# Attention of a two-block kernel: two heads per product, small and large query tiles in turn

## The reference

```
sc = (q_nope . k_nope + q_rope . k_rope) * 96 ** -0.5      # 8 heads, blocks of 128 queries
p = softmax(where(causal, sc, -inf))
out = p @ v                                                # v: 64 columns per head
```

## Time and profile before

| what | value |
|---|---|
| time, median of 3 runs | 2957.47 us (2949.0 to 2968.39) |
| the profiled execution: time, span | 2962.7 us, 2961.0 us |
| busy in the span: PE, DVE, ACT, POOL | 93%, 66%, 46%, 20% |
| attention stage, on the timeline | 1986.8 to 2168.4 us |
| in it, busy: PE, DVE, ACT, POOL | 172.8, 117.9, 89.7, 8.2 us |

### The profile page before, as it was taken

One profiled execution on the slowest core, in us unless ns is written; L12 is line 12 of the kernel. 1 busy time (PEld: TensorE's weight loads), 2 busy tenths in 40 slices (PEclk: granted clock), 3 DMA queues, 4 the chain that ended last, 5 costly groups with the idle time before them and its releaser, 6 DMA issues. The chain is left out here.

```text
span 2961.0 us, 39198 instructions
## 1 busy us (share of the span) xinstructions
PE 2741.1 (93%) x14472; PEld 2268.7 (77%) x14473; DVE 1958.9 (66%) x2494; ACT 1354.4 (46%) x1902; POOL 580.1 (20%) x465
## 2 busy tenths in 40 slices
PE   8999889889979789999999699779999899999998
PEld 7988677777767678888887688657678688888887
DVE  4441167777754689999997843766677888887323
ACT  5111155555542277777776432334455333333312
POOL 0000036555550110000000510320000234331000
PEclk9999989999989799999999899989999899999999
DMA  6446311010007379999997611010031222222314
GB/s 207 178 173 245 113 39 36 36 36 35 27 30 259 128 308 410 409 410 407 411 409 278 186 61 43 1 52 7 0 91 61 64 78 85 85 85 103 140 49 157
DMA packets 165242, 439.27 MB, mean 148 GB/s; under 512 B 21836, under 2 KB 101760, under 8 KB 151808
## 3 DMA queue, kind: packets, MB, share of 16 engines
q1 hardware_dynamic: 150512, 383.60, 35.1%
q0 software_dynamic: 8848, 33.03, 2.9%
q10 hardware_dynamic: 5760, 20.97, 1.7%
HBM read 358.40 MB, written 79.17 MB: 148 GB/s over the span
## 5 line engine op out<-in xcount | busy, mean ns | idle before, releaser
L134 PE MATMUL psum<-part,expert_x_high 128*128 128x512 f32 x520 | 207.0, 398 | 2.9 <-issue 1.5
L136 PE MATMUL psum<-part,expert_x_low 128*128 128x512 f32 x520 | 203.4, 391 | 0.0
L134 PE MATMUL psum<-project_w_high,high 128*128 128x448 f32 (+1 forms) x512 | 194.8, 380 | 3.5 <-DVE low L398 3.5
L135 PE MATMUL psum<-project_w_low,high 128*128 128x448 f32 (+1 forms) x512 | 193.9, 379 | 0.0
L136 PE MATMUL psum<-project_w_high,low 128*128 128x448 f32 (+1 forms) x512 | 193.8, 379 | 0.0
L129 DVE TENSOR_TENSOR expert_down_low<-expert_down,expert_down_high 128x2048 fp32r<-128x2048 f32 x62 | 139.3, 2287 | 39.6 <-ACT expert_down_high L124 39.6
L971 POOL TENSOR_TENSOR mix_ab_step<-mix_abrb,mix_pair_mask 128x512 f32<-128x512 f32 x80 | 116.4, 1479 | 186.1 <-ACT mix_abrb L1106 185.6
L134 PE MATMUL psum<-part,ffn_w_high 128*128 128x512 f32 x352 | 140.5, 399 | 11.6 <-DVE ffn_w_low L129 6.8
L129 DVE TENSOR_TENSOR expert_gate_low<-expert_gate,part 128x2048 fp32r<-128x2048 f32 x64 | 143.8, 2287 | 8.5 <-ACT part L124 7.0
L129 DVE TENSOR_TENSOR expert_up_low<-expert_up,part 128x2048 fp32r<-128x2048 f32 x64 | 143.8, 2288 | 1.0 <-ACT part L124 1.0
L135 PE MATMUL psum<-ffn_b_low,ffn_w_high 128*128 128x512 f32 x352 | 139.1, 395 | 0.0
(11 more groups left out here) (702 smaller groups left out, 7684.7 us busy)
## 6 DMA issues: line engine op xcount, KB each, us to landing
expert_gate<-in_w_gate_dram SPq DMA_DIRECT2D x32, 2048.0 KB, 10.1
expert_up<-in_w_up_dram SPq DMA_DIRECT2D x32, 2048.0 KB, 9.9
expert_down<-in_w_down_dram SPq DMA_DIRECT2D x32, 2048.0 KB, 10.9
ffn_w<-in_ffn_w_up_dram SPq DMA_DIRECT2D x44, 512.0 KB, 4.6
y_rows<-expert_y ACTq DMA_DIRECT2D x32, 512.0 KB, 11.0
hidden_rows<-ffn_hidden SPq DMA_DIRECT2D x20, 512.0 KB, 2.8
ffn_hidden<-hidden_rows SPq DMA_DIRECT2D x20, 512.0 KB, 4.1
down_w<-in_ffn_w_down_dram SPq DMA_DIRECT2D x39, 256.0 KB, 2.6
```

What stands on the lines that cost most here:

```text
L134: pe.matmul(out, left[0], right[0], start=start, stop=False)
L135: pe.matmul(out, left[0], right[1], start=False, stop=False)
L136: return pe.matmul(out, left[1], right[0], start=False, stop=stop)
```

## The change

The turns and their loop are gone; everything is written out. A group is one pair of heads and a pair of tiles, i (SMALL: 1 to 4 blocks) and 7-i (LARGE: 8 to 5 blocks), and has four steps: small tile of head 0, large of head 0, small of head 1, large of head 1. There are 16 groups. For each class c and head u there are buffers of their own (`p`, `p_t`) and banks of their own (small: 0 and 1; large: 2-3 and 4-5). The transposed `p` goes back into the bank its scores came from. A small tile leaves PSUM in one copy of VectorE, a large one in one copy of ScalarE. The value product has the values as weights (128x64) and moves `p_t` (128 columns); the heads of a pair go to partitions 0-63 and 64-127 of one bank, and the result is already in the layout of `feat`. The division must then run along the free axis: GpSimd spreads the two heads' reciprocals over 64 columns each (`spread`), TensorE transposes that (`turn_shares`), ScalarE copies it out (`factor`), and VectorE multiplies into `feat`. `q_now`, `out` and `turn_out` are gone. The scores run two steps ahead.

The core of the diff (waits on the group's first use, and the setup of buffers, are cut):

```diff
+        def of(m):
+            group, r = m // 4, m % 4
+            c, u = r % 2, r // 2
+            i = group % HALF
+            return group, c, u, (i, TT - 1 - i)[c]
+        def score_bank(c, u):
+            return (u, 2 + 2 * u)[c]
...
         @block.gpsimd
-                    pool.tensor_copy(q_now[u][:], q_t[:, ds(j * 2 + u, 1), :].rearrange("p a s -> p (a s)")).then_inc(q_copied[u], 1)
+            for group in range(GROUPS):
+                for c in (SMALL, LARGE):
+                    pool.wait_ge(share_ready[c], group + 1)
...
+                    pool.tensor_copy(spread[c][:], per_row(share[c][:], V_DIM)).then_inc(spread_ready[c], 1)
...
+            def scores(m):
+                if group:
+                    pe.wait_ge(p_t_out[c], of_class(m - 4))
...
+            def turn(m):
+                pe.wait_ge(exp_ready, m + 1)
+                for b in range(i + 1):
+                    last = pe.transpose(bank[score_bank(c, u) + b // 4][:, (b % 4) * P:(b % 4 + 1) * P],
+                                        p[c][u][:, b * P:(b + 1) * P], ident[:])
...
+            def turn_shares(group, c):
+                pe.wait_ge(spread_ready[c], group + 1)
+                pe.transpose(shares(c), spread[c][:].rearrange("p u d -> p (u d)"), ident[:]).then_inc(shares_turned[c], 1)
+            def weigh(group, c):
+                pe.wait_ge(p_t_out[c], of_class(m))
+                pe.wait_ge(shares_copied[c], group + 1)
                 for b in range(i + 1):
-                    last = pe.matmul(bank[6 + m % 2][:, 0:V_DIM], p_t[m % 2][:, b, :],
-                                     values[:, b, ds((j * 2 + u) * V_DIM, V_DIM)], start=(b == 0), stop=(b == i))
+                    for u in range(2):
+                        h = group // HALF * 2 + u
+                        last = pe.matmul(summed(c)[u * V_DIM:(u + 1) * V_DIM, :], values[:, b, h * V_DIM:(h + 1) * V_DIM],
+                                         p_t[c][u][:, b, :], start=(b == 0), stop=(b == i))
+            scores(0)
+            scores(1)
+            for m in range(STEPS):
+                if m + 2 < STEPS:
+                    scores(m + 2)
+                now = (m // 4, SMALL) if m % 4 == 3 else (m // 4 - 1, LARGE) if m % 4 == 0 and m else None
+                if now:
+                    turn_shares(*now)
+                turn(m)
+                if now:
+                    weigh(*now)
...
         @block.scalar
+            def large_out(m):
+                act.wait_ge(turned, m + 1)
+                act.activation(p_t[c][u][:, 0:i + 1, :], three(wide(psum, score_bank(c, u), 2)[:, 0:(i + 1) * P], i + 1), ACT.Copy)\
+                    .then_inc(p_t_out[c], 1)
+            def factors(group, c):
+                act.wait_ge(shares_turned[c], group + 1)
+                act.activation(factor[c][:], shares(c), ACT.Copy).then_inc(shares_copied[c], 1)
+            exps(0)
+            for m in range(STEPS):
+                if m % 4 == 3:
+                    factors(m // 4, SMALL)
+                elif m % 4 == 0 and m:
+                    factors(m // 4 - 1, LARGE)
+                if m + 1 < STEPS:
+                    exps(m + 1)
+                if m % 2 == LARGE:
+                    large_out(m)
...
         @block.vector
+            def shares_of(group, c):
+                v.wait_ge(exp_ready, 4 * group + 3 + c)
+                v.reciprocal(share[c][:], total[c][:]).then_inc(share_ready[c], 1)
+            def finish(group, c):
+                v.wait_ge(made[c], group + 1)
+                v.wait_ge(shares_copied[c], group + 1)
+                v.tensor_tensor(feat[:, group // HALF, i * P:(i + 1) * P], summed(c), factor[c][:], ALU.mult).then_inc(out_done[c], 1)
+            for m in range(STEPS):
+                group, r = m // 4, m % 4
+                if r >= 2:
+                    shares_of(group, r - 2)
+                if m + 2 < STEPS:
+                    bound(m + 2)
+                if r % 2 == SMALL:
+                    small_out(m)
+                if r < 2 and m >= 4:
+                    finish(group - 1, r)
```

More of the change, by code:

```diff
@@ L3200, in attention_stage @@
         future = st.sb("future", [P, P])
[L3201 to L3207, removed]
@@ L3219, in back @@
[L3219 to L3236, removed]
@@ L3239, in attention_stage @@
-        LAST_TURN = (TURNS - 1) * N
-        FROM_BANK = {7: 1, 6: 3, 5: 5, 4: 0, 3: 2, 2: 4, 1: 6, 0: 7}
-        IN_STEP = {N - 3: 7, N - 2: 6, N - 1: 5}
+        p = [[st.sb(f"p{c}{u}", [P, (HALF, TT)[c] * P]) for u in range(2)] for c in range(2)]
+        p_t = [[st.sb(f"p_t{c}{u}", [P, (HALF, TT)[c], P]) for u in range(2)] for c in range(2)]
+        most, bias = ([[st.sb(f"{n}{c}{u}", [P, 1]) for u in range(2)] for c in range(2)] for n in ("most", "bias"))
+        total, share = ([st.sb(f"{n}{c}", [P, 2]) for c in range(2)] for n in ("total", "share"))
@@ new lines, in attention_stage @@
+        spread = [st.sb(f"spread{c}", [P, 2, V_DIM]) for c in range(2)]
+        factor = [st.sb(f"factor{c}", [P, P]) for c in range(2)]
+        const, scored, masked, most_ready, bias_ready, exp_ready, turned = (
+            st.sem(n) for n in "const scored masked most_ready bias_ready exp_ready turned".split())
+        p_t_out, share_ready, spread_ready, shares_turned, shares_copied, made, out_done = (
+            [st.sem(f"{n}{c}") for c in range(2)] for n in (
+                "p_t_out", "share_ready", "spread_ready", "shares_turned", "shares_copied", "made", "out_done"))
@@ new lines, in attention_stage, with head, of_class, summed @@
+        block = st.open()
+        def of(m):
[3 more added lines that the diff above has]
+            return group, c, u, (i, TT - 1 - i)[c]
+        def head(m):
+            return m // (4 * HALF) * 2 + of(m)[2]
+        def of_class(m):
+            return m // 2 + 1
+        def score_bank(c, u):
+            return (u, 2 + 2 * u)[c]
+        def summed(c):
+            return bank[6 + c][:, 0:P]
+        def shares(c):
+            return bank[6 + c][:, 2 * P:3 * P]
@@ L3250, in _ @@
         def _(pool):
[L3251 to L3254, removed]
-                    pool.tensor_copy(q_now[u][:], q_t[:, ds(j * 2 + u, 1), :].rearrange("p a s -> p (a s)")).then_inc(q_copied[u], 1)
+            for group in range(GROUPS):
+                for c in (SMALL, LARGE):
+                    pool.wait_ge(share_ready[c], group + 1)
+                    if group:
+                        pool.wait_ge(shares_turned[c], group)
+                    pool.tensor_copy(spread[c][:], per_row(share[c][:], V_DIM)).then_inc(spread_ready[c], 1)
@@ L3257, in _ @@
         @block.tensor
         def _(pe):
[L3259 to L3263, removed]
+            def scores(m):
+                group, c, u, i = of(m)
+                if group:
+                    pe.wait_ge(p_t_out[c], of_class(m - 4))
+                h = head(m)
                 for n in range(i // 4 + 1):
                     width = min(BANK, (i + 1) * P - n * BANK)
[L3266 to L3275, removed]
+                    last = pe.matmul(bank[score_bank(c, u) + n][:, 0:width], q_t[:, h, i * P:(i + 1) * P],
+                                     k_t[:, h, n * BANK:n * BANK + width], start=True, stop=True)
+                last.then_inc(scored, 1)
+            def turn(m):
+                group, c, u, i = of(m)
+                pe.wait_ge(exp_ready, m + 1)
@@ L3290, in steps @@
[L3290 to L3316, removed]
@@ L3319, in _ @@
+            scores(0)
[9 more added lines that the diff above has]
+                    weigh(*now)
+            turn_shares(GROUPS - 1, LARGE)
+            weigh(GROUPS - 1, LARGE)
         @block.scalar
@@ L3320, in _ @@
         def _(act):
[L3321 to L3337, removed]
+            def exps(m):
+                group, c, u, i = of(m)
+                act.wait_ge(bias_ready, m + 1)
+                if group:
+                    act.wait_ge(turned, m - 3)
+                    act.wait_ge(share_ready[c], group)
+                at = wide(psum, score_bank(c, u), 1 + c)
+                act.activation(p[c][u][:, 0:(i + 1) * P], at[:, 0:(i + 1) * P], ACT.Exp, bias=bias[c][u][:, 0:1], scale=scale,
+                               accum_out=total[c][:, u:u + 1]).then_inc(exp_ready, 1)
@@ L3339, in _, with bound @@
+            exps(0)
[8 more added lines that the diff above has]
+                    large_out(m)
+            factors(GROUPS - 1, LARGE)
         @block.vector
         def _(v):
[L3341 to L3344, removed]
+            def bound(m):
+                group, c, u, i = of(m)
+                at = wide(psum, score_bank(c, u), 1 + c)
+                v.wait_ge(scored, m + 1)
@@ L3372, in _ @@
-            v.wait_ge(const, 16)
-            def steps(j, first, last):
-                for m in range(N):
-                    if after(j, m, last):
-                        bound(*after(j, m, last))
-                    high(j, m)
```

(23 more changed lines are left out.)

71 lines of the change are left out of this document (28 added, 43 removed).

## The result

The changed kernel takes 2934.51 us (median of 6 runs, 2926.26 to 2935.95); the kernel before took 2958.95 beside it. The ratio is 0.9908, 95% interval 0.9888 to 0.9928. The profiled spans are 2961.0 and 2933.1 us, 27.9 apart.

The account below looks back on a forecast made before the run. TensorE's passes bound large tiles, one step's chain small ones. From the first scores 138.6 + 7.3 + 4.0 + 2.8 = 152.7 us against 180.1; with the earlier start 28.5 less, 2957.5 to 2929 us, range 2912 to 2950.

Parts of the forecast that it names:

- The two sides at once: Value products on TensorE: 576 passes at 0.052 us each, 30.0 us instead of 61.6, a gain of 31.6.
- The change of form: TensorE around each `weigh`: 0.10 us more going in and 0.15 coming out, 8.0 us for 32.
- The scores' wait for the copy: scores(m+2) waits for ACT's copy of m-2 from shared banks: 0.67, 0.25, 0 and 0.25 us.
- The weighing's wait for the factor: `weigh` of the large pair waits for `factor`: 0.31, 0.20, 0.09 and 0.42 us.
- GpSimd's spread: 128x128 spread by broadcast on GpSimd: taken at 0.4 us and covered; at 1.04 it would add about 6 us.
- the slow start: First group's eight-block tile at half clock: scores 0.2 + 1.7 + 0.2 + 1.7 cost 4.0 us more.
- The end: From the last transposes: copy 0.9, factor 0.33, `weigh` 1.3 and product 0.3 give 2.8 us, against 4.2 before.
- DVE and ACT: Busy times of the two engines in the stage: DVE 104 us, ACT 93, neither passing TensorE in sum.
- coupled queues: Rival: DVE's and ACT's queue order lets another 0.8 to 1 us wait a group through; 2943 us, chance 0.22.
- ScalarE's and VectorE's copies would become the bound: PSUM copy as the bound, a mechanism placed under the coupling rival: 2943 us, chance 0.22 for the whole rival.
- The clock: Rival: granted clock falls mid-stage; a loss beyond a fifth of the work, 3002 us at half; chance 0.08.
- Not side by side: Rival: heads' value products don't overlap, `weigh` is 61.6 + 8, stage 3 us slower, 2960 us; chance 0.06.

Follow-up runs that it names:

- the run on one side: Changed kernel with the heads' value products one after the other, both on partitions 0 to 63: 2962.14 us, stage 186.1 us.
- spread thrice: Changed kernel with GpSimd making each spread of the shares three times, each waiting for the one before: 2932.65 us, stage 156.5 us.
- the first run: Changed kernel with each value product running all blocks of one head, then all of the other: 2944.17 us, ratio to before 0.9956.

## Why the prediction was right

The forecast was 2929 us, with 28.5 us less by its sum; measured were 2934.5, which is 24.4 under the 2958.95 of before. The sum is of the stage alone, and there 26.1 less stand against its 28.5 (24.7 from the first scores on, forecast 27.4, and 1.4 by the earlier start, forecast 1.1). That the profiled spans are 27.9 apart is closer by chance, with 1.8 from stretches where nothing was changed. Point by point:

- The two sides at once, 31.6 us gained: the pace is 0.0546 instead of the 0.052 read from L1318, so 576 passes are 31.4 us and the gain is 30.2. Shown by the run on one side, 30.6 us.
- The change of form, 0.25 us per weighing: 0.10 in (2044.93 + 0.92 - 0.27 to 2045.78 is 0.20, pace 0.11) and 0.15 out (the last pass of the eight at 2046.165, the scores at 2046.37), as in the earlier trace rows. Missed: the 0.1 in the short row that follows the way out, 1.6 us in all.
- The scores' wait for the copy: forecast 0.67, 0.25, 0, 0.25, measured 0.73, 0.30, 0, 0.29. The weighing's wait for the factor: forecast 0.31, 0.20, 0.09, 0.42, measured 0.30, 0.19, 0.08, 0.41. These come from nothing but the order of issue in each queue and durations of rows. Wrong was to let 1.5 us of drains vanish inside them: the form's change follows the wait. A weighing that waited starts 0.144 us after the factor's copy ends, scores that waited 0.053 us after theirs.
- GpSimd's spread: taken at 0.4 between 0.396 and 1.04 us, measured 0.293, below both. Covered.
- The start: the first scores begin with the stage. A new wait there was overlooked: VectorE's first mask waits 7.4 us for the load of the mask's constants, until 1987.99. It costs nothing in this profile, since TensorE is busy with the scores of the first three tiles at the low clock until 1990.6; in "spread thrice", at full clock, the transposes of the first two tiles wait 1.0 us in all for the exponentials behind it. The four terms of the slow start, put at 4.0, add up to 3.8; the stretch to 1994.80 took 8.59 us where the same rows take 5.07 at full clock, so 3.5.
- The end: 2.8 us from the last transposes were forecast, 3.4 measured (2138.30 to 2141.68); the last group also waits 1.2 us for the spread.
- From the first scores to the end 152.7 us were forecast, 155.5 measured. That it is only 2.8 off is partly luck. A cycle takes 37.58 us where the forecast's terms give 36.48 ((138.6 + 7.3)/4), so four cycles were put 4.4 us too low. Against that, the last group's weighings were counted twice, in TensorE's sum and in the tail: 36 passes and two changes of form, some 2.4 us.
- DVE and ACT were put at 104 and 93 us busy and are at 98 and 85. I had taken sums of single durations from a busy time in which neighbours overlap, and had left in the four copies each of `turn_out`, 2.5 and 2.4 us; nothing hung on it.

Of the rivals: coupled queues did not come, since the look-ahead of two steps held. That ScalarE's and VectorE's copies would become the bound is true to the extent of the waits, 1.3 us a cycle at the scores, and no further. The Trainium skill's "TensorEngine Tiling (Array Packing)", PSUM Bottleneck, warns that the copy may become the bottleneck, there after a speedup of four; this trace, with the value products twice as fast, shows no more of it than these waits. The clock is 1.00 from 1994.5 us to the end of the stage. "Not side by side" was priced at 3 us slower than before; forced by the run on one side it is 4.5 us in the stage (186.1 against 181.6).

## What to carry to other kernels

Where a product's output is 64 partitions wide, put two independent ones on the two halves and let them alternate closely in program order; here it halved the time of 576 passes, while the same passes with one head after the other gave back 60% of it. Gather such rows: each entry and exit together cost 0.25 to 0.35 us, as much as five to six passes. For each buffer, write down the place in each queue at which it is freed and the place at which it is wanted; the copy that is freed in time is not the shortest but the one with nothing ahead of it.

## What the runs showed of the hardware that was not expected

TensorE starts passes of the other half of the array ahead of passes that stand before them in program order, over a reach of three passes (in the first run the second head starts at 2044.723, with three passes of the first still to start, and 28 passes take 23.7 paces). The granted clock over the first 8 us of the stage was anything from 0.53 to 1.00 in profiles of kernels that are identical up to there, and this alone moved the stage's length by up to 2.2 us. And the time of the untouched stages ahead moved by up to 12 us between profiles of kernels that are identical there, more than most of the effects studied here.
